# First projection with a half-direct opening, slots of their own for late modulation units, and a re-cut second attention

## What is computed

```python
# first block
mod = silu(c) @ w_ada + b_ada                       # 6 vectors of 2048: shift, scale, gate, twice
h = rmsnorm(x, norm_mix) * (1 + sc_a) + sh_a
p = h @ w_in                                        # c_q, c_kv, k_pe, q_g, k_g, v_g, z, b, a, gates
y_a = mla(c_q, c_kv, k_pe) @ w_o_mla                # 8 heads, causal softmax
y_b = gated_delta(conv_silu(q_g, k_g, v_g), ...) @ w_o_gdn
x = x + gt_a * ((g_a * y_a + g_b * y_b) @ w_o)
h = rmsnorm(x, norm_ffn) * (1 + sc_f) + sh_f
x = x + gt_f * ((silu(gate) * up) @ w_down)         # width 5632
# second block
a, gate, q, k, v = split(rms_norm(x, pre_mix_g) @ w_in_2)
yc = silu(layer_norm(depthwise_conv31(a * sigmoid(gate))))
s = q @ k.T * 64 ** -0.5 ; s = where(col_mask, s + bias, -1e30)   # 16 heads of 64
ya = softmax(s) @ v
x = x + rms_norm(concat(yc, ya) @ w_out_2, post_mix_g)
x = x + rms_norm(relu(rms_norm(x) @ w_up_2) ** 2 @ w_down_2, post_mlp_g)
```

## Time and profile before

| | us |
|---|---|
| median of 3 runs | 2725.5 |
| the profiled execution | 2724.88 |
| its span, first to last instruction | 2722.8 |
| TensorE busy | 2670.6 (98%) |
| VectorE busy | 1915.2 (70%) |
| ScalarE busy | 1290.7 (47%) |
| GpSimd busy | 140.1 (5%) |

### The profile page before, as it was taken

One profiled execution on the slowest core, in us unless ns is written; L12 is line 12 of the kernel. 1 busy time (PEld: TensorE's weight loads), 2 busy tenths in 40 slices (PEclk: granted clock), 3 DMA queues, 4 the chain that ended last, 5 costly groups with the idle time before them and its releaser, 6 DMA issues.

```text
span 2722.8 us, 39658 instructions
## 1 busy us (share of the span) xinstructions
PE 2670.6 (98%) x15550; PEld 2340.8 (86%) x15550; DVE 1915.2 (70%) x2919; ACT 1290.7 (47%) x1981; POOL 140.1 (5%) x126
## 2 busy tenths in 40 slices
PE   8999999999999999999999999999999999999998
PEld 7788988888898878888888889998888888888887
DVE  6887776877887886565555679996667465575665
ACT  2165643434435444444444554567564444443443
POOL 0000000000011000000000270111200000000000
PEclk9999999999999999999999999999999999999999
DMA  9954366767786786555555555553545555555554
GB/s 387 409 191 155 104 208 209 255 222 235 269 290 229 273 285 220 186 192 188 188 191 187 188 183 173 182 169 128 186 153 192 193 189 193 191 188 193 191 190 146
DMA packets 158731, 565.10 MB, mean 208 GB/s; under 512 B 17616, under 2 KB 21840, under 8 KB 158416
## 3 DMA queue, kind: packets, MB, share of 16 engines
q1 hardware_dynamic: 158544, 562.56, 60.2%
HBM read 560.39 MB, written 2.10 MB: 207 GB/s over the span
## 4 chain that ended last, share of the span: by engine, by line
PE 83%; DVE 9%; DMA 4%; issue 2%; ACT 2%; DVEq 0%; ACTq 0%; SPq 0%
PE BK L369 15%; PE BK L367 15%; PE BK L371 8%; PE BK L366 7%; PE BK L383 7%; PE BK L384 7%; PE BK L387 7%; DVE LO L751 3%; PE BK L376 3%; PE BK L373 3%; PE BK L374 3%; PE BK L398 2%; DMA RAW<-wst_dram 2%; DVE B L993 2%; PE BK L487 1%
## 5 line engine op out<-in xcount | busy, mean ns | idle before, releaser
L587 ACT ACTIVATE HI<-RAW 128x1024 fp32r<-128x1024 f32 x824 | 873.3, 1060 | 1184.5 <-PE BK L367 490.1
L751 DVE TENSOR_TENSOR LO<-RAW,HI 128x1024 fp32r<-128x1024 f32 x824 | 1010.6, 1227 | 360.5 <-ACT HI L587 359.5
L369 PE MATMUL BK<-H,HI 128*128 128x512 f32 x1896 | 750.8, 399 | 0.6 <-DVE H L787 0.4
L367 PE MATMUL BK<-H,HI 128*128 128x512 f32 x1864 | 733.5, 396 | 0.0
L371 PE MATMUL BK<-H,LO 128*128 128x256 f32 x1896 | 528.3, 279 | 13.0 <-DVE LO L751 12.9
L366 PE MATMUL BK<-H,LO 128*128 128x256 f32 x1864 | 520.3, 279 | 0.2 <-DVE H L789 0.2
L371 PEld LDWEIGHTS BK<-H,LO 128*128 128x128 f32 x1896 | 356.5, 188 | 96.1 <-DVE LO L751 20.9
L366 PEld LDWEIGHTS BK<-H,LO 128*128 128x128 f32 x1864 | 350.0, 188 | 80.6 <-DVE H L789 0.6
L369 PEld LDWEIGHTS BK<-H,HI 128*128 128x128 f32 x1896 | 359.7, 190 | 8.0 <-issue 1.7
L383 PE MATMUL BK<-HI,H 128*128 128x512 f32 x896 | 361.4, 403 | 1.0 <-DVE H L789 0.6
L367 PEld LDWEIGHTS BK<-H,HI 128*128 128x128 f32 x1864 | 349.5, 188 | 3.7
(11 more groups left out here) (281 smaller groups left out, 2447.4 us busy)
## 6 DMA issues: line engine op xcount, KB each, us to landing
RAW<-wst_dram SPq DMA_DIRECT2D x837, 512.0 KB, 3.3
RAW<-wada_dram SPq DMA_DIRECT2D x155, 512.0 KB, 4.9
EARLY<-wada_dram SPq DMA_DIRECT2D x37, 512.0 KB, 10.7
EARLY<-wst_dram SPq DMA_DIRECT2D x19, 512.0 KB, 12.1
X<-xT_dram SPq DMA_DIRECT2D x8, 512.0 KB, 7.2
B<-bias_dram SPq DMA_DIRECT2D x32, 128.0 KB, 3.3
out_dram<-B SPq DMA_DIRECT2D x8, 256.0 KB, 2.2
B<-gain_dram SPq DMA_DIRECT2D x1, 1024.0 KB, 4.8
```

The lines of the kernel that those rows point to most:

```text
L367: e.matmul(bk[:, :], hh, H[:, k, :], start=False, stop=last, skip_group_check=True).then_inc(S["tile"], 1)
L369: e.matmul(bk[:, :], hh, H[:, k, :], start=first, stop=False, skip_group_check=True)
L587: e.activation(HI[:, u % NHL, :], raw_at(slot), ACT.Copy).then_inc(S["hi"], 1)
L751: e.tensor_tensor(LO[:, u % NHL, :], raw_at(slot), HI[:, u % NHL, :].bitcast(f32), sub).then_inc(S["lo"], 1)
```

## The change

- The opening (`HALF = 8`): rows 0 to 7 as before. In rows 8 to 15 only the first eight blocks stay direct. The other eight blocks' half banks are put aside to SBUF at row 8 (`put_aside`, ScalarE), and the four banks take eight further blocks (`EARLIER`) as narrow split tiles, rows 0 to 7 of them, two rows of features in each of rows 8 to 11. At row 12 those are put aside too, and the banks take the second half (rows 8 to 15) of the first group. So each row from 8 on has one D and two L units.
- Behind the opening `EARLIER` gets its rows 8 to 15 in narrow blocks of eight tiles; the nine other blocks stay as they were. Evacuation adds the part put aside.
- The last 32 late modulation units get kind B and four slots of their own (`FAR`, in `B1`), from unit 236 at 10 for each 16 units. Zeroing of `B1` and `B2` tiles waits for them.
- `mla_mask` and `na_mask` become a `tensor_tensor_reduce` that also gives the minimum of the negated scores; `soft_max` goes. For that the bias is scaled by one over the norm column on ScalarE (`bias_scaled`), the column mask is put in the bias on the host, and `bias_mask` on GpSimd goes.
- V of the second attention is projected token-major ahead of q and k, two groups, and goes from its banks to `NV` with one ScalarE instruction for each bank (`value_rows`); its transposes go.
- The pieces of the convolution are emitted at paces of 6, 4, 8 and 10 quarters of a pair of taps a unit (a and gate, V, first q and k, the other q and k), and `drain` each 5 tiles.
- `l2norm(0)` begins at lag 52 instead of 64, `gdn` at 90 instead of 96, and the gap of `scalars` is 9 instead of 8.

```diff
+EXTRA, HALF = 8, 8
+FRONT = 2 * HALF + 3 * (16 - HALF)
+FAR_AT, FAR_RATE = 236, 10
+PACE = (6, 4, 8, 10, 5)
-LAT = (3, 0, 3, 12, 8, 24)
+LAT = (3, 2, 3, 12, 9, 24)
...
+            def bias_scaled(i, loaded, factor):
+                q.wait_ge(loaded, factor)
+                e.activation(BB[i % 4], BB[i % 4], ACT.Copy, scale=RI[:, i % 2:i % 2 + 1]).then_inc(S["at_a"], 1)
...
+            def value_rows(g, m, src, done, free):
+                q.wait_ge(done, free)
+                dst = NV[g][:, :, m, :].rearrange("p j (s n) -> p j s n", s=3)[:, :, 0:3:2, :]
+                e.activation(dst, src.rearrange("p (j h n) -> p j h n", j=4, h=2), ACT.Copy, scale=RV[:, m:m + 1]).then_inc(S["at_a"], 1)
...
-            def na_mask(p, ps, i, scores, bias, free):
+            def na_mask(p, ps, i, c, scores, bias, free):
                 q.wait_ge(scores, bias, free)
-                e.scalar_tensor_tensor(p, ps, RQ[:, i % 2:i % 2 + 1], BB[i % 4], mult, add).then_inc(S["at_v"], 1)
+                e.tensor_tensor_reduce(p, ps, BB[i % 4], RQ[:, i % 2:i % 2 + 1], 3e38, add, ALU.min, SM[:, c:c + 1]).then_inc(S["at_v"], 1)
...
-            def soft_max(p, c, masked):
-                q.wait_ge(masked)
-                e.tensor_reduce(SM[:, c:c + 1], p, AX, ALU.max, negate=True).then_inc(S["at_v"], 1)
...
-                kinds += ["D"] * (DIRECT // 8) + ["R"] * (4 if i + ROWS_AHEAD < 16 else 0)
+                kinds += (["D", "D"] if i < HALF else ["D", "L", "L"]) + ["R"] * (4 if i + ROWS_AHEAD < 16 else 0)
...
+                far = 0 if i < FAR_AT else min(32, (i - FAR_AT) * FAR_RATE // 16)
+                kinds += ["L"] + ["A"] * max(0, due - put) + ["B"] * (far - n_far)
...
+            def split_units(k0, first, names, aside=None):
+                u0 = w.tile // 8
+                for u in (u0, u0 + 1):
+                    hi_part(u)
+                    assert st["proc"] == lin_at[u]
+                    proc_next()
+                free = None
+                if aside:
+                    put_aside(aside)
+                    free = [part_tok[n] for n in aside]
+                for u, k in ((u0, k0), (u0 + 1, k0 + 1)):
...
             for r in range(16):
                 while hf_tok[r] is None:
                     next(row_done[0], None)
                 direct_row(r)
+                if r in range(8, 12):
+                    split_units(2 * (r - 8), 0, EARLIER, FIRST[8:] if r == 8 else None)
+                if r in range(12, 16):
+                    split_units(2 * (r - 8), 8, FIRST[8:], EARLIER if r == 12 else None)
                 if r < 15:
                     for i in range(4):
                         row_unit(r + 1, i)
...
+            for n in EARLIER:
+                run(block(H1, h_tok[8:], 8, "w_in", 8, n, ev_qkv(n - 9, None)))
             for n in REST:
                 run(block(H1, h_tok, 0, "w_in", 0, n, ev_qkv(n - 9, n != REST[-1]), wide=n != REST[-1]))
...
+            for g in range(2):
+                for _ in token_blocks(H1, u_tok2, 0, "w_in2", 0, 32 + 4 * g, lambda m: e_v(g, m)):
+                    convolve(PACE[1])
...
             for j in range(1, 8):
-                gen = make2(j)
-                for _ in range(6):
-                    next(gen, None)
-                    next(cg, None)
+                for _ in make2(j):
                     if step < 4 * j:
                         pipe_step(stages, step, 32)
                         step += 1
-                run(gen)
+                    convolve(PACE[3])
```

More of the change, by code:

```diff
@@ L57, in const_array @@
     put("mm", np.where(k <= 128 + s, 0.0, -1e30))
-    start = np.clip(s % 64 - 8, 0, 48)
-    put("nm", np.where((k % 64 >= start) & (k % 64 < start + 16), 0.0, -1e30))
     rot = np.zeros((128, 128), np.float32)
@@ L201 @@
            "at_v", "at_g", "cv_a", "cv_v", "cv_p", "spin")
-LOADS = tuple(f"raw{i}" for i in range(NRAW + NEARLY)) + tuple(f"bias{i}" for i in range(4)) + ("cols", "consts", "x0", "x1", "x2", "x3", "pos", "xr", "gain", "out")
+LOADS = tuple(f"raw{i}" for i in range(NRAW + NEARLY + NLATE)) + tuple(f"bias{i}" for i in range(4)) + ("cols", "consts", "x0", "x1", "x2", "x3", "pos", "xr", "gain", "out")
 def program(nc, xT, pos, cols_d, consts_d, wada, wst, bias_d, gain_d, out, log):
@@ L2100, in walk @@
             mid = now()
+            far_free[0] = mid
             spin(4)
@@ L2418, in drain @@
                     yield
-            later(drain())
+            later(drain(), 0, PACE[4])
             later(cg)
@@ L2659 @@
     dc = np.clip(c[None, :] - c[:, None], -15, 15) + 15
-    bias = I["rpb_2"][0][:, dr[:, None, :, None], dc[None, :, None, :]].reshape(32, 128, 256)
+    left = np.clip(c - 8, 0, 48)[:, None]
+    dc = np.where((c[None, :] >= left) & (c[None, :] < left + 16), dc, 31)
+    table = np.full((16, 15, 32), -1e30, np.float32)
+    table[:, :, 0:31] = I["rpb_2"][0]
+    bias = table[:, dr[:, None, :, None], dc[None, :, None, :]].reshape(32, 128, 256)
     arrays = {
```

207 lines of the change are left out of this document (118 added, 89 removed).

## The result

The changed kernel takes 2706.3 us (median of four runs, 2704.9 to 2707.5) against 2725.0 us for the kernel before, run beside it (2724.5 to 2726.0): a ratio of 0.9931, 95% interval 0.9914 to 0.9948. It is faster by 18.7 us where 14.6 were forecast; 2706.3 lies inside the range of 2697 to 2724 and 4.7 us under the predicted 2711. The profiled execution took 2705.89 us, its span is 2703.9; the one of before took 2724.88 with 2722.8.

The account below looks back on a forecast made before the run. TensorE, busy 2670.6 of 2722.8 us, was taken to set the end, with its idle. Terms of -1, -7, -0.5, -4.4, -2.2, +1.5 and -1 sum to -14.6 us, giving 2711 us, range 2697 to 2724.

Parts of the forecast that it names:

- Part 1: First projection: a longer opening, +19.4 us, against cheaper tiles behind it, -21.5, and +1 of crowding; net -1 us.
- the loop: Opening rows 8 to 15: a VectorE and ScalarE cycle of 9.75 us sets each row, before 7.68; +14.5 us.
- the extras: Opening: putting half banks aside, +0.8 us, and rotary angles with their sines falling partly into the loop, +2 us.
- Part 2: Late modulation units from 880 us on: four own buffers end rounding's waits for loads and most TensorE idle; -7 us.
- The rival, that VectorE's dots stall TensorE: Late modulation units: VectorE's own dots, not slots, stall TensorE, so part 2 gives nothing; 2718 us, chance 0.12.
- Part 3: Attention scores masked and maximum taken in one instruction, bias scaled on ScalarE; -0.5 us, VectorE saving 7 in second attention.
- Part 4: Second attention's V projected token-major: cheaper tiles, 2.6 us, and eight pairs of transposes gone, 1.8; -4.4 us.
- Part 5: Convolution's pace in the second block: -2.2 us at the gates, +1.5 in the second attention, -1 at the output projection.
- The gates' idle: TensorE idle at 1700 to 1740 us, while VectorE's four taps a unit fell behind; three taps save 2.2 us.
- The tail: Around the output projection's start: 5.06 us idle become about 4 with the drain spread wider; -1 us (-4 to +6).
- GpSimd's hold on VectorE: Rival: GpSimd's masking holds VectorE up, and removing it returns at most 30 us of VectorE; 2708 us, chance 0.05.
- The slower case: Rival: VectorE bounds the second attention if the fused instruction costs 0.79 us and every tap 0.51; 2736 us, chance 0.06.

Follow-up runs that it names:

- opening_before: The changed kernel with the first projection of the kernel before, nothing put aside; 2711.7 us.
- shared_old_rate: The changed kernel with late modulation units back in the five buffers shared with the weights, at the old 12 per 16 weight units; 2711.5 us.
- maximum_again: The changed kernel with each second-attention score tile's maximum taken a second time by a separate VectorE reduction; 2710.0 us.
- shared_slots: The changed kernel with late modulation units in the five buffers shared with the weights, still 10 per 16 weight units; 2704.8 us.
- blanks_before: shared_old_rate with the memsets of the second attention's tiles moved back beside the late modulation units; 2712.5 us.
- pace_v8: The changed kernel with four convolution taps a unit instead of two while V is projected; 2710.1 us.
- drain_3: The changed kernel with the second attention's last eight steps handed out every 3 tiles instead of 5; 2709.5 us.

## Why the prediction came out as it did

The way and the range were right; the size was short by 4.1 us (18.7 against 14.6; against the rounded 2711 it is 4.7). Three terms are off by about as much each, two of them one way and one the other (parts 1 and 2 gave 5 and 4 us more, part 5 gave 4 less and a slow clock took 1.6), so that the total came this near is in part luck.

- **Part 1: forecast -1, measured -6.2.** The mechanism stood as written: the loop 9.54 against 9.75, the wait of 1.6 us at the rounding, loads at 408 GB/s, the wide tiles behind it 20.9 to 21.6 us cheaper. Against opening_before the opening cost 16.6 and not 19.4: seven intervals of 9.54 make 1.5 less, and the extras (0.8 for putting banks aside, 2 for the rotary angles) came to 1.5 together. Behind it -20.9 came for -20.5, and 2.0 us in a later stretch that I had left at nothing.
- **Part 2: forecast -7, measured -11.2, and the mechanism half right.** "With four buffers of their own" was one of two cures in the same edit; the runs show either suffices, so the slots are not what the change needed. The rival, that VectorE's dots stall TensorE, fell. The size was short since I read TensorE's idle. A matmul that starts a little late shows no gap, its modelled end covers it. Counting is sharper: from 880 to 1040 us before has 862 matmuls and after 924, and 62 at 0.173 us each (40 / 231) are 10.7 us, against 11.2 measured; shared_old_rate has 883, 41 fewer than after, which by the same price is 7.1 us, against 7.4 measured. 3.8 of the 11.2 us have no cause that a run shows.
- **Part 3: the fused instruction.** I took 0.5 us between bounds of 0.47 and 0.79. From 1779.64 to the next operation at 1780.04 it is 0.40, what the mask alone takes, and the accumulator's read stands beside the next tap. After, VectorE's timeline:

```profile
1779.64 0.47 DVE L918 CUSTOM_DVE_ANT_0 B<-BK,B,SC 128x256 f32<-128x256 f32 x1
1780.04 0.09 DVE L918 DVE_READ_ACCUMULATOR2_ANT SC<- 128x1 f32 x1
1780.04 1.68 DVE L998 SCALAR_TENSOR_TENSOR B<-B,CO 128x256 f32<-128x256 f32 x4
```

  The whole maximum was saved. maximum_again shows that this was worth 3 to 4 us (the second block 3.3 us longer than in after, the median 3.7): without it the second attention is VectorE-bound. What the 16 of the first attention gave (forecast -0.5) no run tells.
- **Part 4, V token-major (-4.4)** was not tried alone. TensorE's busy time in the second block fell from 355.2 to 351.8, by 3.5 us, and to 349.9, by 5.3, in shared_slots, which has the full clock (below); that fits.
- **Part 5: forecast -1.7, measured about +2 (-2.6 + 0.1 + 1.8 + 2.7), and 1.6 of slow clock.** TensorE's idle in the whole second block says the same, 7.8 us before and 9.7 after. The gates' idle went, 2.6 us against 2.2. The second attention, where I charged 1.5, is full (39.88 and 40.00); but 1.7 us came at its first scores, which wait for a bias scaled on ScalarE. I had costed "ScalarE gets 32 scalings" at nothing and did not ask who waits for the first one. The tail is the step that failed in sign. Up to 1920 us before idles 5.06, and its last scores also wait, four times 0.47, for the copy of a transposed tile (`turned`). After idles 7.7: these waits, and besides 1.3 for the convolution's last tap at its first sum, 1.7 for VectorE's root of its norm in front of one step's values, and 1.6 for the low part of an attention row. I had counted tiles of cover for each chain by itself. The drain and the norm share VectorE's queue and, by the code, one ring of banks, and the sum has no term for either. What would undo it the runs don't show: with the norm 19 us sooner it was 7.9 up to 1900, with steps every 3 tiles 8.9, every 7 tiles 7.7. So the norm's place alone is not the cause; which of the two shared things is stays open.
- Of the rivals, GpSimd's hold on VectorE was real at about 3 us in the second attention, and may be part of why the second attention stayed full. The slower case did not come, its first condition failing at once: 0.40, not 0.79 us.

## What to carry to other kernels

Before crediting an edit that gives more buffers, work out the bandwidth that the loads need and what the shared buffers bring; asking a little less often may do the same for nothing. Where a stretch is starved in small waits, count the matmuls in it instead of adding up the idle that the profile shows. Two chains that each have cover enough by themselves may lose it where they meet, in one engine's queue or in one ring of banks, so count them together there. And ask of every operation that changes engines who waits for the first one: here it was 1.7 us of TensorE, and asking for the load one stage sooner took them away. Count what a pace setting really emits before calling an engine safe: here one step of the generator was two taps.

## What the runs showed of the hardware

**The granted clock fell for one short idle, in some executions only.** Windows of 4 us in the tail, after, then shared_slots, with the same work:

```profile
1864.00:1868.00 4.00, 1.83 (x11) 1.16 (x10) 3.89 (x10) 2.37 (x8) 0.00 (x0) 1.00 0.12 33
1868.00:1872.00 4.00, 4.00 (x14) 3.39 (x15) 1.70 (x4) 3.25 (x7) 0.00 (x0) 0.57 0.16 37
...
1864.00:1868.00 4.00, 1.83 (x11) 1.15 (x10) 3.90 (x10) 2.38 (x8) 0.00 (x0) 1.00 0.11 33
1868.00:1872.00 4.00, 3.32 (x20) 2.78 (x20) 1.74 (x5) 3.97 (x8) 0.00 (x0) 1.00 0.19 40
```

Both had TensorE idle for 2.17 of 4 us. In one the next 4 us came at 0.57, mostly the lower level of 1.2 GHz, and gave 14 matmuls in 4.00 busy us; in the other at full clock, 20 matmuls in 3.32. The second block took 361.4 and 359.8 us: that idle costs 1.6 us more when the clock falls, and it looks like busy time. The same fall can cost nothing where TensorE isn't the limit. In the opening TensorE idles 1.85 of 4 us from 56 to 60 in maximum_again and 1.83 in blanks_before; then the clock is 0.62 from 60 to 64 in the first and 1.00 in the second, and the row that starts at 60.0 us takes TensorE 8.83 and 7.14 us. The next row starts at 68.71 and 67.91, but the one behind it at 75.97 and 75.96.

**The same opening took 1.4 us more in some executions.** Row 15 started at 150.5 to 150.8 us in five profiled executions with the opening of after, and at 151.8 to 152.2 in four others. The clock was 1.00 in after, pace_v8 and drain_3, and the loads ran at 402 to 411 GB/s in all of them. In blanks_before and maximum_again the loss is in one place: the last dot of a row, which starts at 56.37 us in after, starts at 57.55 and 57.56, held for the load of its modulation unit, and the later rows keep their distances. One unit takes 1.28 us at 409 GB/s, so it looks as if that load came one unit later; why is open.
